# A two-layer token mixer on one core: the norm of the value rows is spread over ScalarE's and VectorE's other work, the weight ring's first wait moves to a later slot, and the result is stored in five pieces

## The chip, the cores and the metric

The kernel runs on one core of one Trainium2 chip. The metric is the time of one execution in microseconds (us); less is better. A core has TensorE (PE: matmuls, and PEld for weight loads that overlap them), VectorE (DVE), ScalarE (ACT), GpSimd (POOL) and SyncE (SP), which here only issues DMAs. Each engine runs its own instructions in order and waits on semaphores that others raise. All DMAs share 16 DMA engines. On-chip memory is SBUF (the tensor `arena`) and PSUM (8 banks of 128x512 f32, the tensor `psum`).

## The reference, cut to what matters

All of it is float32, with D = 1024 channels and 512 tokens (`SEQ`), plus 256 context tokens (`CTX`). A first block does a norm, a gated delta rule with 8 heads, a second mixer on "value rows", gates and an output projection, and then a convolutional feed-forward. Two attention layers follow. The diff touches the value rows of the first block, the first DMAs and the last one.

```python
def chunk_mlp(u, v, ln_g, ln_b, w_s, b_s):
    v = layer_norm(v, ln_g, ln_b)                       # over the 1024 channels of each token
    vc = v.reshape(bsz, length // A_CHUNK, A_CHUNK, A_GROUPS, A_GW)
    s = jnp.einsum('gij,bnjgc->bnigc', w_s, vc) + b_s.T[None, None, :, :, None]
    return u * s.reshape(bsz, length, A_WIDTH)

u = gelu(p[..., OFF_U:OFF_AV]);  va = gelu(p[..., OFF_AV:OFF_GA])
y_a = chunk_mlp(u, va, a_ln_g, a_ln_b, a_ws, a_bs) @ w_proj_a
```

Before all that, the first block needs `mod = silu(c) @ w_mod` (its first two of six parts) and the norm of x and of the context.

## The kernel before, in words

**The weight ring.** All weights are laid out in one stream of 512 KB slots, and `ring` holds four of them. SP loads slot t into place t % 4 as soon as the semaphore `used` says that PE has freed the slot four earlier (L424 to L427). SP does nothing else until the stream is at its end. Then it waits for the last row of X and stores the whole result, 2 MB, in one DMA (L428 to L430).

**The front.** ACT's queue loads `vecs`, x and the context (`x_in`, 3 MB). PE runs 16 products of the modulation, one ring slot each (L533 to L543). It stops ahead of the third (t == 2) until x_in has landed. Meanwhile ring slots 0 to 5 can be loaded, and no more. ACT squares the 8 tiles of X once x_in is there (L1234), DVE adds them up (L1687), and PE sums them over the partitions inside product 13 (`norm_sums`). After product 15 DVE copies the products' result (L1689), the modulation is transposed and added, and the first tiles of H are formed (L1670, L1222), with which PE goes on.

**The value rows.** PE computes them into 8 PSUM banks (L754 to L764). ACT takes them out with a gelu and sums each row on the way (L1364). DVE makes the negative mean (L1944, L1946). Then ACT squares each of the four row tiles VA[:, tb] around the mean with a row sum (L1371), and takes the root of the variance as exp(-0.5 ln) (L1374, L1376). DVE normalizes each tile with three operations (L1950, L1953, L1955), and forms one more input sum (L1960).

**The mix.** Behind the value rows stand 20 products (N_MIX), each of a 1024x256 weight block with 512 tokens, computed with seven parts instead of eight (Strassen's scheme in Winograd's form). A part is 4 matmuls of 128x128 by 128x256. PE's order (`seven_products`, `last_product`) is: part 1 into bank x, the last part of the product before it, then parts z, y, x, z, x. The helpers of the other engines are:
- `snapshots` on ACT copies bank x, bank z and bank x again to SBUF (L1383, L1387, L1391), since later parts write over them; PE's later parts wait for these copies (semaphore `snap`).
- `mix_joins` on DVE makes three outputs from bank and snapshot (L1918, L1924, L1929); PE's last part waits for all three (`join`), and part z of the next product waits for the first two.
- `weight_sums` on POOL makes four sums of weight blocks (L2602 to L2613), which parts z, x, z, x need (`wsum`).
- In the first four products ACT puts a gelu on the outputs (L1414, L1416, L1397).

On ACT and DVE the whole norm stands ahead of product 0's snapshots and joins. The rows are needed only by PE's `latent_gate` (L766), which runs inside product 3 (gates 0 to 3) and behind the first part of product 4 (gates 4 to 7). Gate g of the last four waits for DVE's operation on gate g - 4 (L1968, semaphore `us`).

**The end.** The last layer's output projection works on two rows of X at a time. DVE adds each result into X (L2477) and counts `b2_xo` up by one for each of the 8 rows.

Of the kernel before, what the change touches and what calls it, by code (L numbers as in the profile page):

```python
# [119 lines left out]
def build(nc, a_stream, a_vecs, a_ident, a_con1, a_con2, a_x, a_ctx, a_ctx2, a_wba, a_lnrows, a_ws, a_bs, a_bias,  # L120
          a_mods, a_conds, a_out):
    ctx = ExitStack()
    with ctx:
# [5 lines left out]
        def s(name):  # L129
            if name not in sems:  # L130
                sems[name] = ctx.enter_context(nc.semaphore(name))
            return sems[name]
# [160 lines left out]
        def vec(name, j=0, n=1):  # L293
            return vecs[:, VEC[name] + j:VEC[name] + j + n]
# [124 lines left out]
        @block.sync  # L419
        def _(sp):  # L420

            for t in range(RING):
                sp.dma_start(ring[:, t, :], a_stream[t]).then_inc(s(f"ring{t}"), 16)
            with sp.Fori(1, T_ALL // RING) as i:  # L424
                for t in range(RING):
                    sp.wait_ge(s("used"), RING * i + t - (RING - 1))
                    sp.dma_start(ring[:, t, :], a_stream[RING * i + t]).then_inc(s(f"ring{t}"), 16)  # L427
            sp.wait_ge(s("b2_xo"), 3 * KT + 8)  # L428
            sp.dma_start(a_out, X[:, :, 0:SEQ]).then_inc(s("stored"), 16)
            sp.wait_ge(s("stored"), 16)  # L430

        def weights(pe, t, i=None, per=0):

# [9 lines left out]
        def _(pe):  # L443
# [88 lines left out]
            pe.wait_ge(s("cond"), 2)  # L532
            for t in range(16):  # L533
                k, hf = divmod(t, 2)
                if t == 2:
                    pe.wait_ge(s("x_in"), 32)
                w = weights(pe, T_PRE + t)
                for j in range(2):
                    r = 32 * (2 * hf + j)
                    m = mm(psum[r:r + 32, 0, :], condp[:, k, :], w[:, SEQ * j:SEQ * (j + 1)], k == 0, k == KT - 1)  # L540
                m.then_inc(s("used"), 1)
                if t == 13:
                    norm_sums(0, (1, 2), True)  # L543
# [656 lines left out]
        def _(act):  # L1200
# [163 lines left out]
                    f(VA[:, tb, hf * SEQ:(hf + 1) * SEQ], psum[:, 4 * hf + tb, :], ACT.Gelu_apprx_tanh,  # L1364
                      accum_out=vsum[:, 2 * tb + hf:2 * tb + hf + 1]).then_inc(s("va"), 1)

            act.wait_ge(s("vmean"), 2)
            for tb in range(XC):
                if tb:
                    act.wait_ge(s("vvar"), tb)  # L1370
                f(vsq, VA[:, tb, :], ACT.Square, bias=vst[:, 1, tb:tb + 1],  # L1371
                  accum_out=vst[:, 2, tb:tb + 1]).then_inc(s("vvar"), 1)
            act.wait_ge(s("vvar"), XC)
            f(vst[:, 3, :], vst[:, 2, :], ACT.Ln, scale=1.0 / D, bias=vec("eps")).then_inc(s("vvar"), 1)  # L1374
            act.wait_ge(s("vvar"), XC + 1)
            f(vst[:, 4, :], vst[:, 3, :], ACT.Exp, scale=-0.5).then_inc(s("vvar"), 1)  # L1376
            def snapshots(n, banks, snaps, w, after=True, ended=None, second=None):

                x, _, z = banks
                if after:  # L1380
                    act.wait_ge(s("join"), 3 * n - 1)
                act.wait_ge(s("seven"), 6 * n + 1)
                f(snaps[0][:, 0:w], psum[:, x, 0:w], ACT.Copy).then_inc(s("snap"), 1)  # L1383
                if ended is not None:
                    ended()
                act.wait_ge(s("seven"), 6 * n + 2)
                f(snaps[1][:, 0:w], psum[:, z, 0:w], ACT.Copy).then_inc(s("snap"), 1)  # L1387
                if second is not None:
                    second()
                act.wait_ge(s("seven"), 6 * n + 4)  # L1390
                f(snaps[2][:, 0:w], psum[:, x, 0:w], ACT.Copy).then_inc(s("snap"), 1)  # L1391

            def mix_ended(n):

                act.wait_ge(s("used"), T_U + 2 * n + 2)
                if n < 4:
                    f(U[:, 2 * n + 1, 0:HALF], psum[:, n % 2, 0:HALF], ACT.Gelu_apprx_tanh).then_inc(s("u"), 1)  # L1397
                elif 8 <= n < 16:
                    to = turn_b[n % 2] if n < 12 else OB[:, 2 * (n - 12) + 1]
                    f(to[:, 0:HALF], psum[:, n % 2, 0:HALF], ACT.Tanh, scale=0.5).then_inc(s("gate_tanh"), 1)  # L1400
                if n == 15:
                    act.dma_start(X[:, :, SEQ:TOK], a_ctx2).then_inc(s("b2load"), 16)

            for n in range(N_MIX):
                snapshots(n, (n % 2, 2, 3), snapsM, HALF, n > 0, (lambda: mix_ended(n - 1)) if n else None)
                if n < 4 or 8 <= n < 16:
                    if n < 4:
                        a, b, how, scale, done = U[:, 2 * n], U[:, 2 * n + 1], ACT.Gelu_apprx_tanh, 1.0, "u"
                    elif n < 12:
                        a, b, how, scale, done = turn_a[n % 2], turn_b[n % 2], ACT.Tanh, 0.5, "gate_tanh"  # L1410
                    else:
                        a, b, how, scale, done = OB[:, 2 * (n - 12)], OB[:, 2 * (n - 12) + 1], ACT.Tanh, 0.5, "gate_tanh"
                    act.wait_ge(s("join"), 3 * n + 2)
                    f(a, a, how, scale=scale).then_inc(s(done), 1)  # L1414
                    act.wait_ge(s("join"), 3 * n + 3)
                    f(b[:, HALF:SEQ], b[:, HALF:SEQ], how, scale=scale)  # L1416
            mix_ended(N_MIX - 1)
            norm_root("1a", ((0, CTX, 4),))
            norm_shift(NORMED["1a"], ((0, CTX, 0),), modT[:, 24:32, :], range(3))
# [199 lines left out]
        def _(dve):  # L1619
# [324 lines left out]
            tt(vst[:, 0, :, None], vs2[:, :, 0:1], vs2[:, :, 1:2], ALU.add).then_inc(s("vmean"), 1)  # L1944
            dve.wait_ge(s("vmean"), 1)
            ts(vst[:, 1, :], vst[:, 0, :], -1.0 / D, None, ALU.mult).then_inc(s("vmean"), 1)  # L1946
            dve.wait_ge(s("vvar"), XC + 2)
            dve.wait_ge(s("mixload"), 16 * 5)
            for tb in range(XC):
                ts(VA[:, tb, :], VA[:, tb, :], vst[:, 1, tb:tb + 1], vst[:, 4, tb:tb + 1], ALU.add, ALU.mult)\  # L1950
                    .then_inc(s("vc"), 1)
                dve.wait_ge(s("vc"), 2 * tb + 1)
                tt(VA[:, tb, :], VA[:, tb, :], lnrows[:, 0, :], ALU.mult).then_inc(s("vc"), 1)  # L1953
                dve.wait_ge(s("vc"), 2 * tb + 2)
                tt(VA[:, tb, :], VA[:, tb, :], lnrows[:, 1, :], ALU.add).then_inc(s("vn"), 1)  # L1955

            modf, adaf = modT.rearrange("p k c -> p (k c)"), adaT.rearrange("p k c -> p (k c)")
            dve.wait_ge(s("vn"), XC)
            dve.wait_ge(s("hsum"), 4 + 3)
            tt(OBm[3], OB4[1][0], OBm[1], ALU.subtract).then_inc(s("hsum"), 1)  # L1960

            def latent_gate(g):

# [7 lines left out]
                dve.wait_ge(s("u"), g + 1 + 4)  # L1971
                tt(U[:, g, :], U[:, g, :], gated, ALU.mult).then_inc(s("us"), 1)

            def mix_joins(n, a, b):

                x = n % 2
                join_first(n, 2, snapsM, a[:, 0:HALF], HALF)
                join_second(n, 3, snapsM, a[:, HALF:SEQ], HALF)
                join_fourth(n, x, snapsM, b[:, HALF:SEQ], HALF)

# [28 lines left out]
            def mix_last(n):  # L2009

                dve.wait_ge(s("used"), T_U + 2 * n + 2)
                add_mix(n, 3, 2 * (n - 16) + 1, turn_b[n % 2], 0, HALF, psum[:, n % 2, 0:HALF])

            for n in range(4):
                mix_joins(n, U[:, 2 * n], U[:, 2 * n + 1])
            for g in range(8):
                latent_gate(g)
            for j in range(4):
# [870 lines left out]
```

## Time and profile before

| | us |
|---|---|
| median of 3 runs (lowest to highest) | 2796.08 (2794.98 to 2800.61) |
| the profiled execution, its own time | 2797.4 |
| its span, first to last instruction | 2795.7 |
| PE busy in the span | 2711.4 (97%) |
| DVE, ACT, POOL busy | 1360.2, 839.9, 836.0 |
| mean granted TensorE clock | 0.993 |
| the store of the result, issue to landing | 7.2 |

The times below are from the profiled execution. Windows and starts are in us from the start of the span. An instruction's group is named by its line, engine and operation with output and inputs. What stands in brackets behind it is the idle time of its engine just before, and who ended it. PE's ends are modelled from its pipeline. The granted clock is a share of 2.4 GHz, and at any moment it is either the whole or half of it (1.2 GHz), so that other values are means over a stretch.

### The profile page before, as it was taken

Reading aid. Unit: us, or ns where it says so; the run is one execution under the profiler, and the core shown is the slowest. Engines: PE = TensorE matmul, PEld = TensorE weight load, DVE = VectorE, ACT = ScalarE, POOL = GpSimd, SP = SyncE. Lnnn points to the kernel's source line nnn. Section 1 sums busy time; section 2 is a strip of 40 time slices with the busy share of each in tenths; the row PEclk is TensorE's granted clock in tenths of the full one; section 3 lists DMA queues with packets and bytes.
Section 4 is the critical chain, followed back from the end, with each engine's and each line's share of the span. In section 5 each row is a group of like instructions: output and inputs, shape, how many; then the busy total and the mean of one; then the engine's idle time right before and its main releaser. Section 6 shows DMA issues by size and latency. Waiting matters only on the chain.

```text
span 2795.7 us, 46448 instructions
## 1 busy us (share of the span) xinstructions
PE 2711.4 (97%) x18476; PEld 2001.8 (72%) x18476; DVE 1360.2 (49%) x2445; ACT 839.9 (30%) x1700; POOL 836.0 (30%) x744
## 2 busy tenths in 40 slices
PE   5899999999979999999999999999999999999998
PEld 2677777777468885888886557765555557778887
DVE  3555555555235555888863136544223512553324
ACT  3344433344221211222111335641111123463220
POOL 0222112222125541555654221013232123103443
PEclk9999999999999999999999999999999999999999
DMA  5111111101313552444422211001111112101222
GB/s 217 55 40 32 43 36 41 38 24 32 135 53 136 181 181 90 151 180 180 158 101 82 79 61 39 2 8 53 60 68 53 61 57 83 54 1 46 91 87 80
DMA packets 61337, 221.42 MB, mean 79 GB/s; under 512 B 6688, under 2 KB 8864, under 8 KB 60896
## 3 DMA queue, kind: packets, MB, share of 16 engines
q1 hardware_dynamic: 42512, 153.11, 15.7%
q0 software_dynamic: 14656, 56.93, 6.0%
q10 hardware_dynamic: 3984, 8.71, 0.9%
q8 instruction: 140, 2.29, 0.3%
q14 instruction: 45, 0.37, 0.0%
HBM read 215.01 MB, written 2.15 MB: 78 GB/s over the span
## 4 chain that ended last, share of the span: by engine, by line
PE 95%; DMA 1%; DVE 1%; ACT 1%; issue 1%; ACTq 0%; SPq 0%; POOL 0%; DVEq 0%; POOLq 0%
PE psum L445 91%; PE psum L945 3%; DMA arena<-in_ctxT 1%; DMA arena<-in_stream 1%; PE psum L681 0%; DVE arena L1953 0%; DVE arena L1955 0%; ACT arena L1371 0%; DVE arena L1950 0%; ACT arena L1342 0%; PE psum L634 0%; ACT arena L1509 0%; ACT arena L1364 0%; DVE arena L2258 0%; ACT arena L1222 0%
## 5 line engine op out<-in xcount | busy, mean ns | idle before, releaser
L445 PE MATMUL psum<-arena 64*64 64x64 f32 (+7 forms) x17676 | 2617.5, 330 | 71.9 <-issue 14.8
L445 PEld LDWEIGHTS psum<-arena 128*128 128x128 f32 (+4 forms) x17676 | 1915.7, 164 | 755.8 <-issue 323.7
L2602 POOL TENSOR_TENSOR arena<-arena 128x512 f32<-128x512 f32 (+1 forms) x99 | 122.2, 1234 | 865.2 <-DMA arena<-in_stream 487.9
L1889 DVE SCALAR_TENSOR_TENSOR arena<-arena 128x1024 f32<-128x1024 f32 x128 | 182.3, 1474 | 0.0
L1918 DVE TENSOR_TENSOR arena<-psum,arena 128x256 f32<-128x256 f32 (+1 forms) x98 | 45.2, 462 | 262.9 <-PE psum L445 254.8
L2606 POOL TENSOR_TENSOR arena<-arena 128x512 f32<-128x512 f32 (+1 forms) x99 | 132.2, 1336 | 100.5 <-PE psum L445 95.2
L1924 DVE TENSOR_TENSOR arena<-psum,arena 128x256 f32<-128x256 f32 (+1 forms) x98 | 45.3, 462 | 218.2 <-PE psum L445 218.2
L2613 POOL TENSOR_TENSOR arena<-arena 128x512 f32<-128x512 f32 (+1 forms) x99 | 137.1, 1385 | 34.7 <-PE psum L445 34.4
L2610 POOL TENSOR_TENSOR arena<-arena 128x512 f32<-128x512 f32 (+1 forms) x99 | 128.9, 1302 | 43.6 <-PE psum L445 37.3
L1391 ACT ACTIVATE arena<-psum 128x256 f32<-128x256 f32 (+1 forms) x98 | 40.8, 416 | 279.5 <-PE psum L445 279.5
L1509 ACT ACTIVATE arena<-psum,arena 128x512 f32<-128x512 f32 (+2 forms) x160 | 115.3, 728 | 30.6 <-DVE arena L2264 17.6
L2569 POOL TENSOR_TENSOR arena<-arena 128x512 f32<-128x512 f32 x16 | 22.2, 1406 | 328.6 <-ACT arena L1298 328.6
L2578 POOL TENSOR_TENSOR arena<-arena 128x256 f32<-128x256 f32 x96 | 76.1, 809 | 133.1 <-PE psum L445 108.3
L1929 DVE TENSOR_TENSOR arena<-psum,arena 128x256 f32<-128x256 f32 (+1 forms) x98 | 45.4, 464 | 109.7 <-PE psum L445 109.4
L945 PE MATMUL psum<-arena 128*128 128x128 f32 x704 | 94.2, 279 | 4.2 <-ACT arena L1509 4.0
L945 PEld LDWEIGHTS psum<-arena 128*128 128x128 f32 x704 | 76.2, 140 | 29.0 <-issue 14.8
L1383 ACT ACTIVATE arena<-psum 128x256 f32<-128x256 f32 (+1 forms) x98 | 40.5, 413 | 178.6 <-PE psum L445 178.3
L1387 ACT ACTIVATE arena<-psum 128x256 f32<-128x256 f32 (+1 forms) x98 | 40.7, 415 | 159.2 <-PE psum L445 159.1
L1314 ACT ACTIVATE arena<-psum 128x256 f32<-128x256 f32 x120 | 46.1, 384 | 137.0 <-PE psum L445 132.3
L1496 ACT ACTIVATE arena<-psum 128x512 f32<-128x512 f32 x104 | 58.8, 596 | 77.1 <-PE psum L945 77.0
L2253 DVE TENSOR_REDUCE arena<-psum 128x2 f32<-128x1536 f32 x32 | 56.2, 1758 | 50.3 <-PE psum L445 50.1
L1337 ACT ACTIVATE arena<-psum,arena 128x128 f32<-128x128 f32 x80 | 25.1, 364 | 101.9 <-PE psum L445 101.9
(270 smaller groups left out, 1837.6 us busy)
## 6 DMA issues: line engine op xcount, KB each, us to landing
arena<-in_stream SPq DMA_DIRECT2D x288, 512.0 KB, 3.7
arena<-in_mods POOLq DMA_DIRECT2D x80, 512.0 KB, 5.7
arena<-gc_rows POOLq DMA_DIRECT2D x16, 384.0 KB, 4.8
arena<-in_bias POOLq DMA_DIRECT2D x16, 384.0 KB, 4.1
arena<-in_xT ACTq DMA_DIRECT2D x1, 2048.0 KB, 17.8
out<-arena SPq DMA_DIRECT2D x1, 2048.0 KB, 7.2
arena<-in_conds ACTq DMA_DIRECT2D x1, 1536.0 KB
arena<-arena POOLq DMA_DIRECT2D x4, 384.0 KB, 4.3
```

Of the source, the lines that this page charges most:

```text
L445: return pe.matmul(out, lhsT, rhs, start=start, stop=stop, skip_group_check=True)
L945: return pe.transpose(out[:, at:at + P], Pr[:, u % 2, at:at + P], ident)
L1314: f(flat(Wt[:, 4 * g:4 * g + 4, :]), psum[:, LB[g], 0:CTX], ACT.Copy).then_inc(s("Wt"), 1)
L1496: f(PT[:, u % 2, at:at + SEQ], score_banks(l, u)[:, at:at + SEQ], ACT.Copy)\
L1509: m = f(Pr[:, u % 2, at:at + w], score_banks(l, u)[:, at:at + w], ACT.Exp, scale=-1.0, bias=st[:, 0, o:o + 1], accum_out=st[:, 1, o:o + 1])
L1889: m = stt(mjunk[:, b % 2, :] if x < len(conds) - 1 else slot, slot, 0.5, cb[:, c, :], ALU.mult, ALU.mult, accum_out=dst(x))
L2253: dve.tensor_reduce(st[:, 0, o:o + 2], x.rearrange("p (a c) -> p a c", a=2), AX_X, ALU.min).then_inc(s("at_mx"), 2)
L2578: pool.tensor_tensor(A[:, 4 * g:4 * g + 4, :], M[:, 4 * g:4 * g + 4, :], level[:, l, g, None, :].to_broadcast([P, 4, HP]), ALU.mult)\
L2602: add(sums[0], a21, a22, ALU.add).then_inc(s("wsum"), 1)
L2606: add(sums[1], sums[0], a11, ALU.subtract).then_inc(s("wsum"), 1)
L2610: add(sums[3], a12, sums[1], ALU.subtract).then_inc(s("wsum"), 1)
L2613: add(sums[2], a11, a21, ALU.subtract).then_inc(s("wsum"), 1)
```

## The change

Four things, in the order of the diff.

1. The result is stored in five pieces: rows 0 and 1, 2 and 3, 4 and 5, then 6, then 7. Each goes once `b2_xo` has counted its rows.
2. PE's wait for x_in stands ahead of product 6 instead of product 2.
3. On ACT, the squares of the value rows are no longer one block. Row 0 is squared between product 0's first and second snapshot, rows 1 and 2 between the second and third, and row 3 behind the third. The root stands behind product 0's gelus.
4. On DVE, the three operations of each row move: row 0 ahead of product 1's joins, row 1 behind its first join, and rows 2 and 3 behind its last. The input sum OBm[3] (L1960) moves behind product 3's joins.

```diff
-            sp.wait_ge(s("b2_xo"), 3 * KT + 8)
-            sp.dma_start(a_out, X[:, :, 0:SEQ]).then_inc(s("stored"), 16)
-            sp.wait_ge(s("stored"), 16)
+            for a, b in ((0, 2), (2, 4), (4, 6), (6, 7), (7, 8)):
+                sp.wait_ge(s("b2_xo"), 2 * KT + b + 8)
+                sp.dma_start(a_out[:, a:b, :], X[:, a:b, 0:SEQ]).then_inc(s("stored"), 16)
+            sp.wait_ge(s("stored"), 16 * 5)
...
-                if t == 2:
+                if t == 6:
                     pe.wait_ge(s("x_in"), 32)
...
-            act.wait_ge(s("vmean"), 2)
-            for tb in range(XC):
+            def row_squares(tb):
+                act.wait_ge(s("vmean"), 2)
                 if tb:
                     act.wait_ge(s("vvar"), tb)
                 f(vsq, VA[:, tb, :], ACT.Square, bias=vst[:, 1, tb:tb + 1],
                   accum_out=vst[:, 2, tb:tb + 1]).then_inc(s("vvar"), 1)
+            def row_root():
...
...
             for n in range(N_MIX):
-                snapshots(n, (n % 2, 2, 3), snapsM, HALF, n > 0, (lambda: mix_ended(n - 1)) if n else None)
+                snapshots(n, (n % 2, 2, 3), snapsM, HALF, n > 0,
+                          (lambda: mix_ended(n - 1)) if n else (lambda: row_squares(0)),
+                          None if n else (lambda: (row_squares(1), row_squares(2))))
+                if n == 0:
+                    row_squares(3)
...
+                if n == 0:
+                    row_root()
...
-            dve.wait_ge(s("vvar"), XC + 2)
-            dve.wait_ge(s("mixload"), 16 * 5)
-            for tb in range(XC):
+            def row_norm(tb):
+                dve.wait_ge(s("vvar"), XC + 2)
                 ts(VA[:, tb, :], VA[:, tb, :], vst[:, 1, tb:tb + 1], vst[:, 4, tb:tb + 1], ALU.add, ALU.mult)\
                     .then_inc(s("vc"), 1)
...
-            dve.wait_ge(s("vn"), XC)
-            dve.wait_ge(s("hsum"), 4 + 3)
-            tt(OBm[3], OB4[1][0], OBm[1], ALU.subtract).then_inc(s("hsum"), 1)
...
-            def mix_joins(n, a, b):
+            def mix_joins(n, a, b, mid=None):
                 x = n % 2
                 join_first(n, 2, snapsM, a[:, 0:HALF], HALF)
+                if mid is not None:
+                    mid()
                 join_second(n, 3, snapsM, a[:, HALF:SEQ], HALF)
                 join_fourth(n, x, snapsM, b[:, HALF:SEQ], HALF)
...
+            dve.wait_ge(s("mixload"), 16 * 5)
             for n in range(4):
-                mix_joins(n, U[:, 2 * n], U[:, 2 * n + 1])
+                if n == 1:
+                    row_norm(0)
+                mix_joins(n, U[:, 2 * n], U[:, 2 * n + 1], (lambda: row_norm(1)) if n == 1 else None)
+                if n == 1:
+                    row_norm(2)
+                    row_norm(3)
+            dve.wait_ge(s("vn"), XC)
+            dve.wait_ge(s("hsum"), 4 + 3)
+            tt(OBm[3], OB4[1][0], OBm[1], ALU.subtract).then_inc(s("hsum"), 1)
+
             for g in range(8):
                 latent_gate(g)
```

## Rows read from the trace of the kernel before

**Rows 1.** The page, part 1: busy time, share of the span, instructions.
```profile
PE 2711.4 (97%) x18476; PEld 2001.8 (72%) x18476; DVE 1360.2 (49%) x2445; ACT 839.9 (30%) x1700; POOL 836.0 (30%) x744
```
**Rows 2.** The chain by time, 760 to 1110 us: start, length, what.
```profile
770.19 2.43 ACT arena L1364 x8
...
778.13 1.28 ACT L1374
...
779.74 1.28 ACT L1376
```
**Rows 3.** Timeline of PE, 755 to 815 us: start, length, operation, idle before.
```profile
754.52 20.82 PE L445 MATMUL psum<-arena 128*128 128x512 f32 x60
781.62 9.19 PE L445 MATMUL psum<-arena 128*128 128x256 f32 x32 [6.27 <-issue]
799.61 15.65 PE L445 MATMUL psum<-arena 128*128 128x256 f32 x64 [8.80 <-DVE arena L1929]
```
**Rows 4.** Timeline of ACT, 755 to 830 us.
```profile
773.05 1.15 ACT L1371 ACTIVATE arena<-arena 128x1024 f32<-128x1024 f32 x1 [0.44 <-DVE arena L1946]
...
803.20 0.39 ACT L1397 ACTIVATE arena<-psum 128x256 f32<-128x256 f32 x1 [2.83 <-PE psum L445]
...
813.63 0.38 ACT L1383 ACTIVATE arena<-psum 128x256 f32<-128x256 f32 x1 [0.91 <-PE psum L445]
...
825.74 0.38 ACT L1383 ACTIVATE arena<-psum 128x256 f32<-128x256 f32 x1 [0.91 <-PE psum L445]
```
**Rows 5.** Timeline of DVE, 740 to 830 us.
```profile
781.28 0.81 DVE L1950 TENSOR_SCALAR arena<-arena 128x1024 f32<-128x1024 f32 x1 [8.26 <-ACT arena L1376]
...
788.73 1.76 DVE L1950 TENSOR_SCALAR arena<-arena 128x1024 f32<-128x1024 f32 x1
790.53 2.17 DVE L1953 TENSOR_TENSOR arena<-arena 128x1024 f32<-128x1024 f32 x1
...
797.24 1.23 DVE L1960 TENSOR_TENSOR arena<-arena 128x1024 f32<-128x1024 f32 x1
```
**Rows 6.** Window behind the second hole: busy (count) by engine, clock, DMA, GB/s.
```profile
800.00:806.00 6.00, 6.00 (x22) 4.99 (x22) 0.00 (x0) 1.14 (x4) 0.00 (x0) 0.76 0.26 76
```
**Rows 7.** Timeline of all engines around the latent gates, 826 to 872 us.
```profile
839.67 1.28 POOL L2613 TENSOR_TENSOR arena<-arena 128x512 f32<-128x512 f32 x1 [0.39 <-PE psum L445]
...
843.08 0.39 ACT L1397 ACTIVATE arena<-psum 128x256 f32<-128x256 f32 x1 [1.28 <-PE psum L445]
...
844.07 0.68 DVE L1968 SCALAR_TENSOR_TENSOR arena<-psum,arena 128x512 f32<-128x512 f32 x1
...
848.38 0.39 ACT L1387 ACTIVATE arena<-psum 128x256 f32<-128x256 f32 x1 [4.91 <-PE psum L445]
```
**Rows 8.** The front: chain, two windows, DMA queues of 14 to 16 us, timeline.
```profile
2.22 20.02 DMA arena<-in_ctxT
...
10.00:22.00 12.00, 0.00 (x0) 0.00 (x0) 0.00 (x0) 0.00 (x0) 0.00 (x0) 1.00 0.98 360
...
22.00:24.00 2.00, 1.72 (x9) 0.40 (x13) 0.86 (x1) 1.58 (x2) 0.00 (x0) 1.00 0.00 0
...
q1 hardware_dynamic: 139, 0.51, 64.6%
q10 hardware_dynamic: 143, 0.29, 38.5%
...
36.19 1.05 PE L445 MATMUL psum<-arena 128*32 128x512 f32 x4 [0.55 <-DMA arena<-in_stream]
...
39.67 3.60 PE L445 MATMUL psum<-arena 128*32 128x512 f32 x16 [0.41 <-DMA arena<-in_stream]
```
**Rows 9.** The end: the store, a window in it, landings of the last ring loads.
```profile
out<-arena SPq DMA_DIRECT2D x1, 2048.0 KB, 7.2
...
2790.00:2791.00 1.00, 0.00 (x0) 0.00 (x0) 0.00 (x0) 0.00 (x0) 0.00 (x0) 1.00 1.01 387
...
DMA to landing us min/median/max: 3.4/3.9/4.6
```

More of the change, by code:

```diff
@@ L1372, in _ @@
                   accum_out=vst[:, 2, tb:tb + 1]).then_inc(s("vvar"), 1)
[L1373 to L1376, printed above, removed]
+            def row_root():
+                act.wait_ge(s("vvar"), XC)
+                f(vst[:, 3, :], vst[:, 2, :], ACT.Ln, scale=1.0 / D, bias=vec("eps")).then_inc(s("vvar"), 1)
+                act.wait_ge(s("vvar"), XC + 1)
+                f(vst[:, 4, :], vst[:, 3, :], ACT.Exp, scale=-0.5).then_inc(s("vvar"), 1)
             def snapshots(n, banks, snaps, w, after=True, ended=None, second=None):
@@ L1946, in _ @@
             ts(vst[:, 1, :], vst[:, 0, :], -1.0 / D, None, ALU.mult).then_inc(s("vmean"), 1)
-            dve.wait_ge(s("vvar"), XC + 2)
-            dve.wait_ge(s("mixload"), 16 * 5)
-            for tb in range(XC):
+            modf, adaf = modT.rearrange("p k c -> p (k c)"), adaT.rearrange("p k c -> p (k c)")
+            def row_norm(tb):
+                dve.wait_ge(s("vvar"), XC + 2)
                 ts(VA[:, tb, :], VA[:, tb, :], vst[:, 1, tb:tb + 1], vst[:, 4, tb:tb + 1], ALU.add, ALU.mult)\
@@ L1955, in _ @@
                 tt(VA[:, tb, :], VA[:, tb, :], lnrows[:, 1, :], ALU.add).then_inc(s("vn"), 1)
-            modf, adaf = modT.rearrange("p k c -> p (k c)"), adaT.rearrange("p k c -> p (k c)")
-            dve.wait_ge(s("vn"), XC)
-            dve.wait_ge(s("hsum"), 4 + 3)
-            tt(OBm[3], OB4[1][0], OBm[1], ALU.subtract).then_inc(s("hsum"), 1)
             def latent_gate(g):
```

## The prediction

> **What bounds the kernel now.** First the page: TensorE (PE) is busy 97% of the span [rows 1]. So only stretches in which PE waits can be shortened by this diff, which takes no matmul away. Second, the chain of waits in order of time, where it leaves PE: from 770 us on it goes through ScalarE (ACT), L1364 to L1376 [rows 2], then VectorE (DVE), L1950 to L1960 [rows 5]. The PE timeline shows what that costs: two holes, 6.27 and 8.80 us, with 9.19 us of matmuls between them [rows 3].
>
> What is lost there is more than the holes. One part (four matmuls, 128x256) is a seventh of a product; the first snapshots of products 2 and 3 are at 813.63 and 825.74 [rows 4], so a product takes 12.11 us and a part 1.730 us. From the last value-row matmul (770.17, start of L1364 [rows 2]) to the end of product 2's first part (813.6) PE does 14 parts, 6 of product 0, 7 of product 1 and 1 of product 2. At full rate: 14 x 1.730 = 24.2 us, end at 794.4. Lost: 813.6 - 794.4 = 19.2 us. Two holes explain 15.1. The rest is the clock: behind the second hole the granted clock averages 0.76, a mix of 2.4 and 1.2 GHz [rows 6], and the part that ends at 803.20 [rows 4] took 3.6 us from 799.61 [rows 3] where 1.73 is usual.
>
> Third, the front: PE waits for x_in until 22.24 [rows 8]. Fourth, the end: one store of 2 MB, issued when DVE has finished the last row, lands 7.2 us later [rows 9].
>
> **Spread norm, ACT.** The work is the same: four squares of 1.15 us plus accumulator read, 1.25 to 1.28 apart, then Ln and Exp with a table load of 1.28 each (778.13 to 781.25) [rows 2, 4]. I place it on the unhindered PE clock, where product 0's parts end at 771.9, 773.6, 775.4, 777.1, 778.8 and 780.55. Snapshot 1 goes at 772.6, row 0's square 773.05 to 774.3, snapshot 2 to 774.7, rows 1 and 2 to 777.2, snapshot 3 to 777.6. PE wants snapshot 1 at 775.4, 2 at 777.1 and 3 at 778.8: each is there, so the squares cost nothing; uncovered, each would cost 1.25. Row 3's square ends at 778.9, the two gelu at about 781.4, the root (3.1 us) at 784.6. Behind it on ACT stand product 1's first snapshot (785.0; PE wants it at 787.5) and the gelu with its table reload (786.7), then the second (787.1; wanted at 789.2). Slack 2.1 us or more; cost nothing.
>
> The trace has two loads in the root, L1374 and L1376, for Ln and Exp [rows 2]. The Trainium skill ("ScalarE: Activation LUTs", section "Table sets: the hidden batching unit") says that ln then exp needs one load, since one set holds both. Here the trace disagrees; by the page the root would end 1.3 us earlier, and the sum would gain at most the 0.2 us taken below for a late join.
>
> **Spread norm, DVE.** A row is three operations, 0.81 + 1.23 + 1.23 = 3.3 us, or 1.76 + 2.17 + 2.17 = 6.0 while GpSimd's (POOL) weight sums run beside it [rows 5]. New order on DVE: all joins of product 0 by 781.0 (before, at 799); row 0 from 784.6 to 787.9; join 1 of product 1 (PE ready 787.5); row 1; join 2 (791.0); join 3 (792.7); rows 2 and 3. Queued behind row 1 are the joins that PE's last part of product 1 needs at 794.4. POOL's sums of product 2 start near 789 (their two slots come free at 784.0, are issued by 784.9 and land 3.4 us later at the earliest [rows 9]). So row 1 takes 5.1 (mixed) to 6.0: it ends at 793.4 to 794.3, join 3 at 794.2 to 795.1, against 794.4. Cost 0 to 0.7, I take 0.2. Rows 2 and 3 end at 801 to 806; PE wants product 2's second join at 808 and the rows, for its latent gates, at 811. Covered.
>
> The subtraction L1960 (1.23 us [rows 5]) moves behind product 3's joins, ahead of DVE's latent gates. On PE gates 4 to 7 run from 843.08 to 848.38 less one part of 1.73, so 0.89 each, gate 7 from about 845.8; it needs the DVE operation of 844.07, which ends at 844.75 [rows 7]. Slack 1.0, new delay 1.15, or 2.1 if POOL's sum at 839.67 [rows 7] stretches it. Cost 0.15 to 1.1; I take 0.7, nearer the upper end, since that POOL row starts within the same microsecond.
>
> Sum for this part: 19.2 - 0.2 - 0.7 = 18.3 us (17.4 to 19.1).
>
> **Weight ring's wait, second to sixth product slot.** PE no longer stops with slots 2 to 5 loaded; it uses them as they land, and SyncE refills four more (2.1 MB) before x_in. The DMA engines are full until 22 us (0.98) and idle in 22 to 24 (0.00) since PE has freed no slot; while full they serve the weights and x packet for packet: 139 and 143 packets, 0.51 and 0.29 MB, in 2 us, together 0.40 MB/us [rows 8]. The four slots get at least an equal share, so all 2.1 MB stand ahead of x_in, which comes 2.1 / 0.40 = 5.2 us later (4.4 if part of x goes first, 5.9 at the 0.36 MB/us of 10 to 22 us [rows 8]): at 27.4. The pattern behind x_in then repeats four products further on: product 11 started 13.9 us behind x_in (36.19 [rows 8]), so product 15 can at 41.3, and takes 0.9 to 1.05. It ends at 42.3 where 13 to 15 with the norm's sums end at 43.27 now (39.67 + 3.60 [rows 8]): gain 1.0 us, range -0.4 to 1.9. The squares on ACT and their sums on DVE, eight tiles after x_in, are done by 37, before product 13 wants them. The queue it moves past is SyncE's, issued in order; nothing else waits in it.
>
> The Trainium skill ("DMA: Bandwidth & Descriptors", sections "Queues, rings and completion order" and "Issuing engines are not separate DMA queues") says that the queues share 16 engines, which take turns between them packet by packet, so that more weights in flight are time taken from x. By that rule, the trace agrees.
>
> **Store in five pieces.** SyncE issues the pieces behind its last ring loads, while PE still works on the last two products (24 us), so the first three lie beside matmuls, and row 6's has the 3 us of PE's last part and DVE's last row. The last piece, 256 KB, starts when the whole store did. Of the 7.2 us, 2.10 MB at 387 GB/s are 5.4; 1.8 is fixed, so 256 KB need 1.8 + 0.7 = 2.5; a ring load of twice the bytes lands in 3.4 at least [rows 9]. Bounds 2.5 and 3.4, I take 2.6, nearer the row of the same operation: gain 4.6 (3.8 to 4.7). The last ring loads stand ahead of the pieces, so they aren't delayed.
>
> The Trainium skill (the same page, section "Rules for kernel authors") speaks against pieces: coalesce many small transfers into one large one. Paid one after another, five fixed parts of 1.8 us would be 9 us; but four of them lie beside matmuls, and no run here shows them yet.
>
> **Sum.** 18.3 + 1.0 + 4.6 = 23.9 us. The profiled execution took 2797.4 (span 2795.7 and 1.7 around it): 2773.5. It lies 1.3 above the median of the runs, 2796.08, so the forecast for the median is 2772.2.
>
> **Rivals.**
> (a) DVE becomes the late one (0.12): rows 0 and 1 both run at the slow 6.0 us. Join 1 at 791.0, row 1 to 797.0, join 3 at 797.8: PE waits 3.4, and the clock falls again (1.9, as behind the second hole). Part one gives 13.2 in place of 18.3: 2777.3. For it: the slow rows are real [rows 5]. Against: POOL has nothing to do at 784.6 until slots land.
> (b) The store's pieces bring nothing (0.05), each small one landing as late as the whole: 2776.8. Against: the ring's 3.4.
> (c) x_in comes later than its bytes say (0.05), by 3 us more, since x is served after the weights: front -2, 2775.2.
> (d) x_in isn't delayed (0.03), and the full 4.3 us of idle DMA is recovered: 2768.9. Against: equal packet counts [rows 8].
> (e) The change doesn't do what it says (0.04): the work only moves, the joins wait behind it and PE waits as long as before; part one gives 0 and the store 4.6: 2791.5.
> (f) Slower (0.03). The row work on two in-order queues blocks every join: PE waits for the root (3.1), for four slow rows (24.0), and the clock falls four times (7.6), 34.7 us where 19.2 were lost; less the store's 4.6 it is 2807. It decides once new waits of PE pass 23.8 us (29.4 for slower by over 0.2%). Against: products 2 and 3 give DVE 10 us of idle time each.
>
> **How the numbers follow.** Forecast 0.68, own range 2769.5 to 2775.5. With (a), (b), (c) the range is 2769 to 2778.5, some 0.85, allowing for what the first case misses. About 0.2% (5.6 us) is what a measurement of this kernel can tell from no change. Faster: all but (e) and (f), 0.93; same 0.04; slower 0.03.
>
> **What would show it.** In the trace after: no PE hole over 1 us between the value rows' end and product 4, granted clock 1.00 there; DVE's row operations in two groups, some at 2.2 us; two table loads for the root and one back; x_in landing at 27 and no idle DMA before it; out's last piece at 2.4 to 3.4 us. A PE wait on L1929 near product 1 or inside gates 5 to 7 would show costs too small here; x_in landing at 22 to 24 would make the front term wrong.

## The result, and the profile after

The changed kernel takes 2773.28 us (median; 2772.49 to 2775.34) against 2795.53 for the kernel before on the same chip. The ratio is 0.9918, with a 95% interval of 0.9902 to 0.9933: faster by 22 us, 0.8%. The forecast was 2772.2. The profiled execution has a span of 2771.2 us against 2795.7.

The page of the kernel after, part 1 (busy time, share of the span, instructions), answers [rows 1]. PE is busy as long as before, 2711 us, in a span that is 24.5 us shorter:

```profile
PE 2711.1 (98%) x18476; PEld 2000.4 (72%) x18476; DVE 1351.9 (49%) x2445; ACT 839.3 (30%) x1700; POOL 834.4 (30%) x744
```

Line numbers have moved: L1365 is the gelu of the value rows, L1373 a square, L1379 and L1381 the root, L1389, L1393 and L1397 the snapshots, L1930, L1936 and L1941 the joins, L1963, L1966 and L1968 a row's norm, L2034 the input sum that was L1960, L1976 DVE's operation for a latent gate that was L1968 before, L1403, L1424 and L1426 the gelus of the mix, L2622 to L2633 POOL's weight sums.

**The mix.** The chain of waits of the kernel after, 760 to 1110 us (start, length, what), answers [rows 2]. It no longer leaves PE at 770 but at 820:

```profile
759.94 60.16 PE psum L446 x271
...
820.47 2.06 DVE arena L2034
822.53 0.61 DVE arena L1976
...
827.26 191.35 PE psum L446 x888
```

The timeline of PE, 765 to 830 us, answers [rows 3]: one unbroken stretch where two holes were, and then three short waits, all for L1976.

```profile
764.50 59.94 PE L446 MATMUL psum<-arena 128*128 128x512 f32 x284
824.60 1.13 PE L446 MATMUL psum<-arena 128*128 128x128 f32 x8 [0.16 <-DVE arena L1976]
825.93 1.13 PE L446 MATMUL psum<-arena 128*128 128x128 f32 x8 [0.20 <-DVE arena L1976]
827.26 3.07 PE L446 MATMUL psum<-arena 128*128 128x128 f32 x17 [0.20 <-DVE arena L1976]
```

The timeline of ACT, for [rows 4]: snapshots and squares take turns, and the root with its two table loads stands behind product 0's gelus.

```profile
769.86 0.60 ACT L1365 ACTIVATE arena<-psum 128x512 f32<-128x512 f32 x1 [25.08 <-PE psum L446]
...
772.15 0.40 ACT L1389 ACTIVATE arena<-psum 128x256 f32<-128x256 f32 x1
772.72 1.15 ACT L1373 ACTIVATE arena<-arena 128x1024 f32<-128x1024 f32 x1 [0.16 <-DVE arena L1958]
...
782.73 1.28 ACT L1381 ACT_TABLE_LOAD   x1
784.02 0.21 ACT L1381 ACTIVATE arena<-arena 128x4 f32<-128x4 f32 x1
784.14 0.37 ACT L1389 ACTIVATE arena<-psum 128x256 f32<-128x256 f32 x1
784.52 1.28 ACT L1403 ACT_TABLE_LOAD   x1
...
794.13 0.38 ACT L1389 ACTIVATE arena<-psum 128x256 f32<-128x256 f32 x1 [0.70 <-PE psum L446]
```

The timeline of DVE, for [rows 5]: row 1 between the first and second join of product 1, partly at the slow rate (2.18), the third join over at 792.8; and the moved input sum at 2.06.

```profile
787.52 0.42 DVE L1930 TENSOR_TENSOR arena<-psum,arena 128x256 f32<-128x256 f32 x1
787.85 0.81 DVE L1963 TENSOR_SCALAR arena<-arena 128x1024 f32<-128x1024 f32 x1
788.69 1.23 DVE L1966 TENSOR_TENSOR arena<-arena 128x1024 f32<-128x1024 f32 x1
789.95 2.18 DVE L1968 TENSOR_TENSOR arena<-arena 128x1024 f32<-128x1024 f32 x1
792.05 0.41 DVE L1936 TENSOR_TENSOR arena<-psum,arena 128x256 f32<-128x256 f32 x1
792.38 0.41 DVE L1941 TENSOR_TENSOR arena<-psum,arena 128x256 f32<-128x256 f32 x1
...
820.47 2.06 DVE L2034 TENSOR_TENSOR arena<-arena 128x1024 f32<-128x1024 f32 x1
822.45 0.68 DVE L1976 SCALAR_TENSOR_TENSOR arena<-psum,arena 128x512 f32<-128x512 f32 x1
```

A window of the kernel after (columns as in [rows 6]: the third from the end is the granted clock) shows 1.00 where the old holes had left 0.76:

```profile
788.00:794.00 6.00, 6.00 (x29) 5.24 (x29) 5.90 (x7) 1.32 (x3) 5.00 (x3) 1.00 0.01 3
```

**The front**, for [rows 8]: the chain, and two windows. x_in lands at 27.27 instead of 22.24, the DMA engines are now busy from 10 to 24 us (DMA share 1.03), and DVE copies the products' result (L1701, before L1689) at 42.61 instead of 43.32. The clock that the first window prints, 0.99, is too high; why is told with e3 and e4.

```profile
2.22 25.05 DMA arena<-in_ctxT
...
42.61 0.70 DVE arena L1701
...
58.47 0.61 ACT arena L1239
...
10.00:22.00 12.00, 5.71 (x16) 0.67 (x16) 0.00 (x0) 0.00 (x0) 0.00 (x0) 0.99 1.03 401
22.00:24.00 2.00, 0.00 (x0) 0.00 (x0) 0.00 (x0) 0.00 (x0) 0.00 (x0) 0.50 1.03 390
```

**The end**, for [rows 9]: all five pieces from issue to landing, and the last two from the list of DMA issues of 2700 to 2800 us.

```profile
DMA to landing us min/median/max: 2.0/2.8/6.8
...
out<-arena SPq DMA_DIRECT2D x2, 256.0 KB, 2.1
```

Four stretches can be read from any trace of this kernel, and the experiments are judged by them. *Copy*: start of DVE's copy in the front. *Mix*: from the first gelu of the second half of the value rows to product 5's first snapshot. *Rest*: from there to DVE's last operation. *Tail*: from the start of DVE's last operation to the end of the span.

| trace | copy | mix | rest | tail |
|---|---|---|---|---|
| before | 43.32 | 86.89 | 1930.47 | 8.2 |
| after | 42.61 | 68.99 | 1929.41 | 3.0 |

### The profile page after: what moved, and what is told of

It reads as the page before. It is cut to its first block, busy times and chain, and to the rows that moved or that the text cites. A ratio compares the mean times of both kernels' runs of the same rounds, so it can differ in the third digit from the quotient of the medians.

```text
span 2771.2 us, 46454 instructions
## 1 busy us (share of the span) xinstructions
PE 2711.1 (98%) x18476; PEld 2000.4 (72%) x18476; DVE 1351.9 (49%) x2445; ACT 839.3 (30%) x1700; POOL 834.4 (30%) x744
## 4 chain that ended last, share of the span: by engine, by line
PE 96%; DMA 1%; DVE 1%; ACT 1%; issue 1%; ACTq 0%; POOL 0%; SPq 0%; DVEq 0%; POOLq 0%
PE psum L446 93%; PE psum L946 3%; DMA arena<-in_ctxT 1%; PE psum L682 0%; DMA arena<-in_stream 0%; ACT arena L1343 0%; PE psum L635 0%; DVE arena L1976 0%; ACT arena L1521 0%; DVE arena L2278 0%; ACT arena L1223 0%; DVE arena L2034 0%; DVE arena L2292 0%; DVE arena L2273 0%; ACT arena L1338 0%
## 5 line engine op out<-in xcount | busy, mean ns | idle before, releaser
L2622 POOL TENSOR_TENSOR arena<-arena 128x512 f32<-128x512 f32 (+1 forms) x99 | 124.2, 1255 | 856.0 <-DMA arena<-in_stream 443.2
L1901 DVE SCALAR_TENSOR_TENSOR arena<-arena 128x1024 f32<-128x1024 f32 x128 | 175.8, 1422 | 0.0
L1930 DVE TENSOR_TENSOR arena<-psum,arena 128x256 f32<-128x256 f32 (+1 forms) x98 | 45.2, 461 | 251.8 <-PE psum L446 244.5
L1936 DVE TENSOR_TENSOR arena<-psum,arena 128x256 f32<-128x256 f32 (+1 forms) x98 | 45.3, 462 | 220.4 <-PE psum L446 220.2
L2633 POOL TENSOR_TENSOR arena<-arena 128x512 f32<-128x512 f32 (+1 forms) x99 | 139.5, 1409 | 35.2 <-PE psum L446 34.9
L1397 ACT ACTIVATE arena<-psum 128x256 f32<-128x256 f32 (+1 forms) x98 | 40.7, 415 | 278.3 <-PE psum L446 278.2
L1941 DVE TENSOR_TENSOR arena<-psum,arena 128x256 f32<-128x256 f32 (+1 forms) x98 | 45.4, 463 | 113.6 <-PE psum L446 113.3
L946 PEld LDWEIGHTS psum<-arena 128*128 128x128 f32 x704 | 76.1, 141 | 29.0 <-issue 14.8
L1389 ACT ACTIVATE arena<-psum 128x256 f32<-128x256 f32 (+1 forms) x98 | 40.4, 412 | 178.5 <-PE psum L446 178.2
L1393 ACT ACTIVATE arena<-psum 128x256 f32<-128x256 f32 (+1 forms) x98 | 40.6, 414 | 158.7 <-PE psum L446 158.4
```

What stands on the lines that cost most here:

```text
L946: return pe.transpose(out[:, at:at + P], Pr[:, u % 2, at:at + P], ident)
L1901: m = stt(mjunk[:, b % 2, :] if x < len(conds) - 1 else slot, slot, 0.5, cb[:, c, :], ALU.mult, ALU.mult, accum_out=dst(x))
L2622: add(sums[0], a21, a22, ALU.add).then_inc(s("wsum"), 1)
L2633: add(sums[2], a11, a21, ALU.subtract).then_inc(s("wsum"), 1)
```

## The experiments

### One part at a time

e1_store_only has the five pieces and nothing else of the change.

```diff
-            sp.dma_start(a_out, X[:, :, 0:SEQ]).then_inc(s("stored"), 16)
+            for a, b in ((0, 2), (2, 4), (4, 6), (6, 7), (7, 8)):
+                sp.wait_ge(s("b2_xo"), 2 * KT + b + 8)
+                sp.dma_start(a_out[:, a:b, :], X[:, a:b, 0:SEQ]).then_inc(s("stored"), 16)
```

> Only the store of the kernel after, everything else as before. Theory: what counts is the last piece of 256 KB, which the trace after shows landing in 2.0 to 2.1 us where the whole store took 7.2; gain 5.1 us, ratio 0.9982. Rival (the pieces bring nothing, because the gain of that trace is in the mix): ratio 1.000 and a tail of 7 us behind the last VectorE operation.

Measured: ratio 0.9979 (0.9970 to 0.9988), tail 3.0 us, mix 87.30. The tail is as short as in the kernel after: the store's gain is 5.2 us, and the rival falls.

e2_norm_only has ACT's and DVE's new order alone (the parts 3 and 4 of the change).

```diff
-                if t == 6:
+                if t == 2:
...
-            for a, b in ((0, 2), (2, 4), (4, 6), (6, 7), (7, 8)):
...
+            sp.dma_start(a_out, X[:, :, 0:SEQ]).then_inc(s("stored"), 16)
```

> Only the spread norm, with the front and the store of before. Theory: 19.2 us of lost PE time come back less 1.26 us of waits at the latent gates: gain 17.9 us, ratio 0.9936, and the gates stretch shows the same three PE waits on L1976. Rival (part of what the trace after shows between 857 us and the end, 1.1 us, belongs to the norm as well): gain 19 us, ratio 0.9932.

Measured: ratio 0.9933 (0.9919 to 0.9947), or 18.7 us of 2797.66; mix 69.00, the kernel after to 0.01; tail 8.1. So the norm gives 17.9 us where it was meant to. The totals don't separate 17.9 from 19; the rest is 1929.56, and e12 below shows how little that says.

e3_front_only has PE's wait at product 6 alone; e4_no_front is the kernel after with the wait back at 2.

```diff
-                if t == 2:
+                if t == 6:
                     pe.wait_ge(s("x_in"), 32)
```

> Only PE's wait for x_in at product 6. Theory: x_in lands near 27.3, product 15 ends near 42.6 (0.7 us earlier than before), and the granted clock is 0.5 from 22 to 38 us and again at 46 to 52, so that the first heads' products give the 0.7 us back: PE's next hand-over to ScalarE (start of L1238) at 58.3 to 58.6 against 58.27; total within 0.5 us of before. Rival (the clock in that stretch varies from run to run and has nothing to do with the wait): clock 1.0 there and start of L1238 at 57.6.

> The kernel after with the wait put back at product 2. Theory: the front's change is worth nothing; total within 0.5 us of the kernel after (2773), clock 1.0 until 48 us and start of L1238 near 58.3. Rival (the front is worth the 0.7 us of its products or more): 0.7 to 1 us slower than after. Rival (the colder clock costs more than the wait gives): 0.5 to 1 us faster than after.

Measured: e3 0.9999 (0.9990 to 1.0008) with x_in at 27.33, copy at 42.18 and the next hand-over to ACT (start of L1238) at 56.97. e4 0.9918 (0.9904 to 0.9931), copy at 44.20, hand-over at 59.72. For 46 to 54 us the theory that the late wait makes the clock cold is wrong: the granted clock averages 0.57 there in e4, with the wait at 2, and 0.79 in e3, with the wait at 6. For 22 to 40 us it does go with the wait: 0.53 to 0.66 in the six traces with the wait at 6, 0.74 to 0.87 in the six with it at 2. What the wait gains at the copy is net of that.

The 1.00 that the windows of before print for 10 to 22 us [rows 8] is not a reading. The first record of the clock in that trace is at 31.42 us, and a window counts what has no record as full. PE's timeline of before tells the level. One product's four matmuls take 1.05 us from 31.95 on, while two products took 3.17 just before, with no wait between them:

```profile
28.05 3.17 PE L445 MATMUL psum<-arena 128*32 128x512 f32 x8 [2.12 <-DMA arena<-in_stream]
31.95 1.05 PE L445 MATMUL psum<-arena 128*32 128x512 f32 x4 [0.73 <-DMA arena<-in_stream]
```

So PE ran at the lower level up to the first record, and the means for 22 to 40 us above count it so. The kernel after is alike: its first record is at 15.03 us, and four such matmuls took 1.92 at 11.33 and 1.05 at 15.77.

All traces with the wait at 2 or at 6:

| wait at product | copy, each trace | mean | hand-over, each trace | mean |
|---|---|---|---|---|
| 2 (before, e1, e2, e4, e10, e12) | 43.32 42.50 44.44 44.20 44.25 43.18 | 43.65 | 58.27 57.34 60.13 59.72 59.91 58.58 | 58.99 |
| 6 (after, e3, e5, e6, e7, e8) | 42.61 42.18 42.15 42.14 43.24 42.78 | 42.52 | 58.47 56.97 58.34 57.62 59.34 57.74 | 58.08 |

The later wait is worth 1.1 us at the copy, with a standard error of 0.4 by the scatter of the traces. The 0.9 at the hand-over has one of 0.6 and is not shown. From copy to hand-over takes 14.8 to 15.0 us where the clock of 46 to 54 us is 0.79 and 15.4 to 16.2 where it is 0.57 to 0.67, and both occur with either wait. The pair of traces read first (0.7 us ahead at the copy, 0.2 behind at the hand-over) had one of each kind. The totals are too coarse for 1 us.

### The cover of DVE's work

e5_sub_early puts the input sum behind row 3's norm, where DVE has time.

```diff
                 if n == 1:
                     row_norm(2)
                     row_norm(3)
+                    dve.wait_ge(s("vn"), XC)
+                    dve.wait_ge(s("hsum"), 4 + 3)
+                    tt(OBm[3], OB4[1][0], OBm[1], ALU.subtract).then_inc(s("hsum"), 1)
-            dve.wait_ge(s("vn"), XC)
-            dve.wait_ge(s("hsum"), 4 + 3)
-            tt(OBm[3], OB4[1][0], OBm[1], ALU.subtract).then_inc(s("hsum"), 1)
```

> The kernel after, with the input sum OBm[3] (one 128x1024 subtraction) right behind row 3's norm instead of behind product 3's joins. Theory: its 2.1 us stood between the joins and the operations that PE's latent gates wait for, and cost 1.26 us there. From the value rows' end to product 5's first snapshot: 68.99 us in the kernel after, 67.7 here; no PE wait on L1976. Product 2's first join comes 1.2 us later than in the kernel after and is waited for by nobody. Rival (the gates wait for something else, such as the weight sums of POOL): 69.0 again. The other rival: the late first join now holds PE, and the stretch is 69 or more.

Measured: mix 67.72, and no wait of PE is left in it. PE's timeline of e5, 765 to 850 us, is one line:

```profile
764.48 85.75 PE L446 MATMUL psum<-arena 128*128 128x512 f32 x420
```

So the moved subtraction cost 1.27 us, and the cost can be had back. The median is 2770.14 us, ratio 0.9906 (0.9889 to 0.9922). The same edit gives 67.97 and 67.73 in e10 and e11; the 0.2 us more in e10 is the late join told below.

e8_two_rows_mid takes the cover away: rows 1 and 2 both stand ahead of product 1's second join.

```diff
-                mix_joins(n, U[:, 2 * n], U[:, 2 * n + 1], (lambda: row_norm(1)) if n == 1 else None)
+                mix_joins(n, U[:, 2 * n], U[:, 2 * n + 1], (lambda: (row_norm(1), row_norm(2))) if n == 1 else None)
                 if n == 1:
-                    row_norm(2)
                     row_norm(3)
```

> The kernel after with rows 1 and 2 both between product 1's first and second join on VectorE, instead of row 1 there and row 2 behind the joins. Theory (VectorE's cover was near its edge): row 2 adds 5.5 us, product 1's third join ends near 798.3 on the kernel after's time scale where PE wants it at 794.0; PE waits 4.3 us, and its clock falls to 1.2 GHz behind the wait and costs up to 1.9 more: from the value rows' end to product 5's first snapshot 73.3 to 75.2 us against 68.99. Rival (joins have room, since PE can go on with the next product): 69.0.

Measured: mix 76.23, 7.2 us over the kernel after; median 2779.44. In e8's timelines PE waits 5.12 us for the third join, and a window behind the wait has a clock of 0.68:

```profile
798.07 32.53 PE L446 MATMUL psum<-arena 128*128 128x256 f32 x160 [5.12 <-DVE arena L1941]
...
798.00:804.00 6.00, 5.93 (x19) 4.98 (x20) 3.09 (x3) 1.53 (x5) 0.00 (x0) 0.68 0.15 25
```

Of the 7.2 us, 5.1 are the wait. The clock behind it is 0.50 up to 801.8 us, 3.7 us in which PE does half its work, and so accounts for 1.9 of the other 2.1. The theory holds, though the 76.23 lies above its 73.3 to 75.2, mostly by the wait. Here a hole of 5 us on PE costs 7.

### The store

e6_store_8 stores each row by itself, e7_store_2 rows 0 to 6 together and then row 7.

```diff
-            for a, b in ((0, 2), (2, 4), (4, 6), (6, 7), (7, 8)):
+            for a, b in ((0, 7), (7, 8)):
```

> The kernel after with the store in eight pieces of one row each. Theory: only the last piece counts, and it has the same 256 KB; from the start of the last VectorE operation to the end of the span 2.9 us as in the kernel after. Rival (every piece pays its fixed part, many small transfers are worse than one): each of the three further pieces adds up to 2 us to the tail.

> The kernel after with the store in two pieces, rows 0 to 6 (1.8 MB) and row 7. Theory: the first can only go when row 6 is ready, 3.4 us ahead of the last; at 387 GB/s its bytes take 4.7 us behind 1.3 us of start-up, so it is still moving when the last is issued, and the last queues behind it: tail of 2.9 + 2.6 to 3.5 us, some 5.5 to 6.4. Rival (the pieces don't disturb each other): tail 2.9 to 4.

Measured: e6 tail 3.0, as with five pieces. e7 tail 4.6. The issues of e7 in 2760 to 2771 us:

```profile
out<-arena SPq DMA_DIRECT2D x1, 1792.0 KB, 6.3
out<-arena SPq DMA_DIRECT2D x1, 256.0 KB, 3.7
```

The same 256 KB take 3.7 us behind a large piece that is still moving, 2.1 behind one that has landed. So the last piece does queue behind the bytes ahead of it, as the theory had it. The tail stayed under its 5.5 to 6.4, because I had added the small piece's start-up to the large one's, and they overlap: issued 3.2 us apart, the two land 0.6 us apart. Eight pieces in place of five don't hurt.

### The dose at the front

e9_wait_at_10 and e11_sub_early_wait_8 move the wait further; e10_sub_early_no_front is e5 with the wait at 2.

```diff
-                if t == 6:
+                if t == 10:
                     pe.wait_ge(s("x_in"), 32)
```

> The kernel after with PE's wait for x_in at product 10 instead of 6. Theory: four more ring slots (2.1 MB) pass ahead of x at 0.40 MB/us, so x_in lands 5.2 us later still, near 32.4; its squares are done 9.3 us behind it at 41.7, and product 13's norm sums and products 14 and 15 wait for that: VectorE's copy (start of L1701) at 44.4 against 42.1 to 43.2 with the wait at 6 and 42.5 to 44.4 at 2. Rival (more room for the weights is always better, since the ring is what bounds the front): x_in near 27.3 and the copy at 40 to 41.

> The kernel after with the early input sum of e5 and the wait for x_in back at product 2. Theory: the later wait is worth about 1 us of the front, so this is 0 to 2 us slower than e5 (2770), hardly to be told from it, with VectorE's copy at 42.5 to 44.4. Rival (the later wait is worth nothing): the same copy time as in e5, 42.2.

> The kernel of e5 with the wait at product 8. Theory: x_in at 27.3 + 2.6 = 29.9, squares done at 39.2, product 13's norm sums at 40.1, products 14 and 15 by 41.9: VectorE's copy at 41.9, 0.2 to 1 us earlier than at 6; total within 1 us of e5, 2770. Rival (the ring's restart behind x_in costs more when fewer products are left to hide it): copy at 43 or later.

Measured: x_in lands at 22.15 to 22.4 us with the wait at 2, 27.3 to 27.5 at 6, 29.9 at 8 and 32.46 at 10. Each slot of 512 KB that passes ahead delays x_in by 1.28 us, to be read as 0.41 MB/us. e9's copy is at 46.71, later than expected (44.4), and its median is 2775.31, ratio 0.9924 (0.9908 to 0.9941). PE's timeline of e9 shows why:

```profile
32.51 3.64 PE L446 MATMUL psum<-arena 128*32 128x512 f32 x16 [6.14 <-DMA arena<-in_ctxT]
41.82 4.79 PE L446 MATMUL psum<-arena 128*128 128x512 f32 x12 [5.67 <-DVE arena L1699]
```

The norm sums wait for the squares until 41.82, as expected. But the sums and the last two products then take 4.79 us, not 2.7, since the clock is 0.50 in 40 to 46 us behind that wait. e11 has its copy at 42.48 (expected 41.9), no better than the wait at 6 (42.15 to 43.24), and a median of 2769.57 us, ratio 0.9904 (0.9887 to 0.9920). e10 has its copy at 44.25 and 2774.47 us, ratio 0.9924 (0.9908 to 0.9941). e5 and e11 have the lowest medians of all kernels run, 3 to 4 us under that of the kernel after, though from other sessions. The intervals of the ratios overlap; what tells the two from it is the mix, 1.3 us.

### The same kernel twice

e12_before_again is the kernel before, unchanged.

> The kernel before, traced once more. Theory: two traces of one kernel differ by 1 to 3 us in the front and the heads, where the granted clock's mean in 46 to 54 us is 0.57 or 0.79, and by less than 0.5 us from the value rows' end to product 5's first snapshot (86.89) and in the tail (8.15). Rival (a trace is exact everywhere, and the 1.1 us that the kernel after gained between product 5 and the end come from the change): the stretch from product 5's first snapshot to the last VectorE operation is 1930.5 again within 0.2.

Measured: copy 43.18, mix 87.40, rest 1928.02, tail 8.2. The mix repeats within 0.5 us and the tail within 0.1, but the rest is 2.45 us shorter with not a line changed. The 1.1 us that the kernel after seemed to gain there need no cause.

## Why the prediction was right, point by point

| term of the sum | forecast (bounds) | traces |
|---|---|---|
| lost PE time that comes back | 19.2 | 19.2 up to product 2 |
| late join of product 1 | -0.2 (0 to -0.7) | 0 in after, -0.2 in e6, e7 and e10 |
| input sum ahead of the gates | -0.7 (-0.15 to -1.1) | -1.3 |
| wait for x_in | 1.0 (-0.4 to 1.9) | 1.1 at the copy |
| store | 4.6 (3.8 to 4.7) | 5.2 |
| sum | 23.9 | 24.2 |

**Lost time at the full clock.** Product 2's first snapshot comes 24.27 us after the value rows (794.13 - 769.86), where 14 parts at 1.730 us are 24.2. Measuring the loss against the full rate, and not as the sum of the two holes, was the step that counted: the holes alone would have said 15.1. Of the other 4.1 us the forecast named only the clock behind the second hole. Windows of before show it behind both:

```profile
781.60:785.70 4.10, 4.08 (x10) 3.29 (x11) 4.00 (x5) 0.49 (x2) 0.19 (x1) 0.50 0.02 4
799.60:802.80 3.20, 3.19 (x8) 2.57 (x9) 0.00 (x0) 0.77 (x3) 0.00 (x0) 0.50 0.00 0
```

In 4.1 and 3.2 us of matmuls at half the clock PE loses 3.65 us. The other 0.5 is not traced.

**The squares on ACT.** The placement was right within 0.5 us: snapshot 1 at 772.15 (forecast 772.6), the root over at 784.2 (784.6), with two table loads in it; 0.3 us of either is that the value rows end earlier in this trace. The Trainium skill's one load for ln and exp ("ScalarE: Activation LUTs", "Table sets: the hidden batching unit") isn't what this program does, before or after.

**The rows on DVE.** Row 1 took 4.3 us, below the 5.1 to 6.0, since only its last operation ran slow. Its second, from 788.69, took its usual 1.23, though POOL's first sum of product 2 ran beside it. It was POOL that was slow there, as its timeline in the kernel after shows:

```profile
788.85 2.19 POOL L2622 TENSOR_TENSOR arena<-arena 128x512 f32<-128x512 f32 x1 [7.29 <-PE psum L446]
```

In e6, e7 and e10 POOL's sum starts first, by 0.02 to 0.1 us (in e6 at 789.22 against 789.26). It then takes 1.27, and DVE's operation 2.25 to 2.33. Which of the two starts first thus decides which has its full speed. In these three traces row 1 takes 5.3 to 5.4 us, within the forecast, the third join ends 24.0 us after the value rows, PE's next matmul starts 0.15 us behind it, and the mix is 0.2 us longer. So the late join of the forecast is real and costs 0.2 us, in some runs. Rival (a) needed rows 0 and 1 both slow; of their six operations one was, or two in those traces. That a row too many there costs 7.2 us was shown by e8, so the price of that rival was real and its condition was not met.

**The input sum.** This term was mis-sized: 1.27 us (e5), above the bound of 1.1. The mechanism was the forecast one. The subtraction starts 0.3 us after POOL's last weight sum for product 4 and takes 2.06 instead of 1.23. The timelines of POOL and of DVE in the kernel after have the sum, and the operation that gate 7 waits for:

```profile
820.17 1.27 POOL L2633 TENSOR_TENSOR arena<-arena 128x512 f32<-128x512 f32 x1 [0.39 <-PE psum L446]
...
826.43 0.68 DVE L1976 SCALAR_TENSOR_TENSOR arena<-psum,arena 128x512 f32<-128x512 f32 x1
```

What was off is the slack of 1.0 us for gate 7. I had read PE's times from ACT's copies, which come 0.2 us behind PE. PE's single matmuls in the trace of before start gate 4 at 842.88 and gate 7 at 845.56, and PE starts 0.15 us after DVE's operation has ended (827.11 and 827.26 in the kernel after). So the slack was 0.66 us. DVE's operation for gate 7 starts 1.19 us behind gate 4 in before and 3.04 behind it in the kernel after, 1.85 later: 1.2 us past the slack, nearly all of the 1.27. Gates 5 and 6 wait as well and start at DVE's pace of 1.33 us, where [rows 7] gave PE 0.89 a gate, but this adds nothing: gate 7's start is set by its own operation of DVE. The profile books only 0.56 us as waits. The Trainium skill ("SBUF — State Buffer", section "SBUF: two separate sides") says that POOL and a DVE operation with two SBUF inputs lock the port that they share, the first keeps it to its end, and the other is blocked. The trace agrees: POOL's sum has its full speed and ends at 821.44, and the subtraction ends 1.1 us behind it, at 822.53, about the time it takes alone. Row 1 agrees as well, with DVE first in the kernel after and POOL first in e6.

**The front.** x_in was forecast for 27.4 and came at 27.27; the copy was forecast at 42.3 and came at 42.61. Equal packets of both queues were the right reading, e9 and e11 confirm it at two more doses, and rival (d) falls. Not forecast was how much the clock in the first 60 us varies from run to run. It adds up to 1.4 us to a stretch of 15 and hides the gain in any single pair of traces.

**The store.** Mis-sized on the low side: 256 KB landed in 2.0 to 2.1 us, below my lower bound of 2.5. The bound came from 387 GB/s, the rate of the middle of the transfer, for all 2 MB, which left 1.8 us for the fixed part. Both landings together (7.2 and 2.05 us) give 1.84 MB in 5.15 us, 0.36 MB/us, and a fixed part of 1.3. The Trainium skill's advice to coalesce ("DMA: Bandwidth & Descriptors", "Rules for kernel authors") would have kept the one store; five or eight pieces cost nothing here, since only the last stands on the path, and e7 shows the one thing to mind, that the piece before must have landed.

**The rivals.** (b) falls with the tail of 3.0 us, (c) and (d) with x_in at 27.3, and (e) and (f) with PE's unbroken stretch; (a) is told above.

**The total** by these terms is 24.2 us, by the two profiled spans 24.5 and by the medians 22.3, with an interval of the ratio that spans 19 to 27 us. The rest, which differed by 2.45 us between two traces of one kernel, is more than that gap.

## What to carry to other kernels

Price a hole on TensorE against the full rate across the whole stretch, with the work behind it, since the clock is lost as well: here 19.2 us for 15.1 us of holes. Work that another engine does in one block can be cut up between its short duties at no cost, as long as each piece ends before the next hand-over that TensorE waits for; find the operation with the least slack and look at what else runs on POOL then, because an operation of DVE with two SBUF inputs takes 2.06 to 2.33 us instead of 1.23 here when POOL's has started first. For the end of a kernel only the last piece of a store counts, if those before it have landed.

## What the runs showed that I had not expected

- The granted clock at the start varies between runs in which PE does the same. With the wait at product 2, PE idles from 9 to 22 us. The first record of the clock, at the full level, is at 9.1 to 9.7 us in four of these traces (e1, e2, e4, e10), at 24.9 in e12 and at 31.4 in before, which are one kernel. What sets it is open.
- A window's mean clock is only good behind the trace's first record of the clock: ahead of it 1.00 is printed, while the matmuls run at half that pace.
- One stretch can tell 0.3 us, while the whole can't tell 2: the mix lies within 68.99 to 69.21 in six traces that share its code, and the 1930 us behind it differ by 2.45 us in two traces of one kernel.
- A store of 256 KB to HBM lands 2.0 us after its issue with nothing ahead of it, and 3.7 with a piece of 1.8 MB, issued 3.2 us earlier, still moving.
